# Attention scores: the low-key rotary product as two 64-row matmuls for two neighbouring score banks

## The reference, cut to what matters

```python
def mla_branch(cq, ckv, kr, z, g_q, w_uq, g_kv, w_ukv, cos, sin):
    ...
    def attend(blk):
        qn_i, qr_i = blk
        s = jnp.einsum('bqhd,bkhd->bhqk', qn_i, kn) + jnp.einsum('bqhr,bkr->bhqk', qr_i, kr)
        p = jax.nn.softmax(s.astype(jnp.float32), axis=-1).astype(v.dtype)
        return jnp.einsum('bhqk,bkhd->bqhd', p, v)
```

## Time and profile before

| | |
|---|---|
| median of 3 runs | 3331.22 us (3323.81, 3331.22, 3331.67) |
| the profiled execution, its time | 3325.03 us |
| its span in the profile | 3323.2 us |
| PE busy | 3091.8 us, 93% of the span |
| DVE, ACT, POOL busy | 41%, 35%, 20% |
| scores, first to last start of L1567 | 912.9 us to 1550.6 us |
| L1567 to L1571 | 256 matmuls each |

### The profile page before, as it was taken

One profiled execution on the slowest core, in us unless ns is written; L12 is line 12 of the kernel. 1 busy time (PEld: TensorE's weight loads), 2 busy tenths in 40 slices (PEclk: granted clock), 3 DMA queues, 4 the chain that ended last, 5 costly groups with the idle time before them and its releaser, 6 DMA issues.

```text
span 3323.2 us, 48512 instructions
## 1 busy us (share of the span) xinstructions
PE 3091.8 (93%) x17652; PEld 2611.1 (79%) x17652; DVE 1373.4 (41%) x2428; ACT 1158.3 (35%) x2089; POOL 655.4 (20%) x597
## 2 busy tenths in 40 slices
PE   4899999766899999999996999989999999999999
PEld 4668888656778888888786888868888888877887
DVE  5377777533567676775324111112222222222111
ACT  3552245433245555554225111123332333222110
POOL 2111211064212121221221000012121221112221
PEclk8999999887899999999998999999999999999999
DMA  6233354572411121211553111122121212135321
GB/s 216 77 118 99 111 165 157 202 232 63 116 36 57 45 60 42 63 51 59 170 165 127 70 73 73 47 79 76 57 76 57 76 57 76 57 109 170 101 89 62
DMA packets 261517, 318.50 MB, mean 96 GB/s; under 512 B 16851, under 2 KB 195283, under 8 KB 257908
## 3 DMA queue, kind: packets, MB, share of 16 engines
q1 hardware_dynamic: 261398, 316.89, 29.2%
HBM read 214.07 MB, written 102.76 MB: 95 GB/s over the span
## 4 chain that ended last, share of the span: by engine, by line
PE 83%; DVE 4%; POOL 3%; issue 3%; DMA 3%; ACT 3%; SPq 1%; POOLq 0%; DVEq 0%; ACTq 0%
PE PS L325 11%; PE PS L326 11%; PE PS L327 11%; PE PS L2117 4%; PE PS L2118 4%; PE PS L2119 4%; PE PS L2222 4%; PE PS L2224 3%; PE PS L2223 3%; PE PS L1578 3%; PE PS L1600 2%; PE PS L1601 2%; PE PS L1602 2%; PE PS L1567 2%; PE PS L2360 2%
## 5 line engine op out<-in xcount | busy, mean ns | idle before, releaser
L325 PE MATMUL PS<-hTh,whi 128*128 128x512 f32 x1664 | 660.9, 397 | 28.1 <-DVE hTl L281 14.5
L326 PE MATMUL PS<-hTl,whi 128*128 128x512 f32 x1664 | 652.0, 392 | 0.0
L327 PE MATMUL PS<-hTh,wlo 128*128 128x512 f32 x1664 | 651.9, 392 | 0.0
L325 PEld LDWEIGHTS PS<-hTh,whi 128*128 128x128 f32 x1664 | 315.2, 189 | 102.5 <-issue 18.1
L327 PEld LDWEIGHTS PS<-hTh,wlo 128*128 128x128 f32 x1664 | 315.1, 189 | 66.9
L326 PEld LDWEIGHTS PS<-hTl,whi 128*128 128x128 f32 x1664 | 315.5, 190 | 63.2
L317 POOL TENSOR_TENSOR whi<-wraw,zero 128x1024 fp32r<-128x1024 f32 x52 | 99.9, 1922 | 981.1 <-PE PS L327 953.0
L2117 PE MATMUL PS<-ow_h,of_h 128*128 128x512 f32 x576 | 225.0, 391 | 7.6 <-DVE oy L2074 7.6
L2118 PE MATMUL PS<-ow_l,of_h 128*128 128x512 f32 x576 | 224.8, 390 | 0.0
L2119 PE MATMUL PS<-ow_h,of_l 128*128 128x512 f32 x576 | 224.7, 390 | 0.0
L1676 ACT ACTIVATE pth<-PS 128x512 fp32r<-128x512 f32 x256 | 153.6, 600 | 187.5 <-PE PS L1578 187.5
(11 more groups left out here) (251 smaller groups left out, 6018.1 us busy)
## 6 DMA issues: line engine op xcount, KB each, us to landing
projT<-pev SPq DMA_DIRECT2D x80, 256.0 KB, 2.6
xt<-x SPq DMA_DIRECT2D x8, 2048.0 KB, 9.0
mw<-wmod SPq DMA_DIRECT2D x64, 256.0 KB, 2.8
oxt<-x SPq DMA_DIRECT2D x32, 512.0 KB, 4.8
sg_v<-vev SPq DMA_DIRECT2D x64, 256.0 KB, 2.3
wraw<-wuz SPq DMA_DIRECT2D x32, 512.0 KB, 5.9
vm<-sg_v SPq DMA_DIRECT2D x16, 1024.0 KB, 5.6
sgT<-mT SPq DMA_DIRECT2D x16, 1024.0 KB, 4.4
```

Source lines behind the costliest of these rows:

```text
L325: pe.matmul(PS[:, bank, :], w[1][:, s, k, :], hTh[:, k, b], start=(k == 0), stop=False)
L326: pe.matmul(PS[:, bank, :], w[1][:, s, k, :], hTl[:, k, b], start=False, stop=False)
L327: mm = pe.matmul(PS[:, bank, :], w[2][:, s, k, :], hTh[:, k, b], start=False, stop=(k == KD - 1))
```

## The change

`qsl` gets a fourth slice: the high part of the rotary query in both halves of the partitions. In the place of the fifth matmul of every bank stand, once for each pair of banks (0 and 1, 2 and 3), two matmuls of 64 rows: rows 0 to 63 into the even bank, rows 64 to 127 into the odd bank. They open the accumulation of both banks. So PE waits for the exponentials of both banks before the even one. The four other matmuls of a bank stay, and the fourth now releases `s_S`. The product low·low of the rotary parts is left out.

POOL gets a fourth instruction for each query block, and the counts of `s_q` go from 3 to 4. `qsl` grows by a third and moves to the place of `cql`, whose last reader comes before.

```diff
-        qsl = at("qsl", M0 + 165 * K, [P, 2, 3, P], F32R)
+        qsl = at("qsl", M0 + 64 * K, [P, 2, 4, P], F32R)
...
-                pe.wait_ge(s_q, N * 3 + 9)
+                pe.wait_ge(s_q, N * 4 + 12)
                 for b in banks:
-                    pe.wait_ge(s_exp, N * 4 + b + 1)
                     o, c = PS[:, b, :], blk(b)
-                    pe.matmul(o, qsl[:, u, 0, :], kh[:, c], start=True, stop=False)
+                    if b % 2 == 0:
+                        pe.wait_ge(s_exp, N * 4 + b + 2)
+                        for e in range(2):
+                            r = slice(ROPE * e, ROPE * e + ROPE)
+                            pe.matmul(PS[:, b + e, :], qsl[r, u, 3, :], krl[r, blk(b + e)], start=True, stop=False)
+                    pe.matmul(o, qsl[:, u, 0, :], kh[:, c], start=False, stop=False)
                     pe.matmul(o, qsl[:, u, 0, :], kl[:, c], start=False, stop=False)
                     pe.matmul(o, qsl[:, u, 1, :], kh[:, c], start=False, stop=False)
-                    pe.matmul(o, qsl[:, u, 2, :], krh[:, c], start=False, stop=False)
-                    pe.matmul(o, qsl[:, u, 2, :], krl[:, c], start=False, stop=True).then_inc(s_S, 1)
+                    pe.matmul(o, qsl[:, u, 2, :], krh[:, c], start=False, stop=True).then_inc(s_S, 1)
...
                 pool.wait_ge(s_S, N * 4 + 4)
-                pool.tensor_tensor(qsl[:, u, 0:3:2, :], qraw[:, u, :, :],
+                pool.tensor_tensor(qsl[:, u, 0:4:3, :], qraw[:, u, :, :],
                                    zero[:, 0:1].unsqueeze(1).broadcast_to([P, 2, P]), ALU.add).then_inc(s_q, 1)
-                pool.wait_ge(s_q, N * 3 + 7)
+                pool.wait_ge(s_q, N * 4 + 9)
+                pool.tensor_tensor(qsl[0:ROPE, u, 2, :], qraw[0:ROPE, u, 1, :],
+                                   zero[0:ROPE, 0:1].broadcast_to([ROPE, P]), ALU.add).then_inc(s_q, 1)
+                pool.wait_ge(s_q, N * 4 + 10)
                 pool.tensor_tensor(qsl[:, u, 1, :], qraw[:, u, 0, :], qsl[:, u, 0, :].bitcast(F32), ALU.subtract).then_inc(s_q, 1)
-                pool.wait_ge(s_q, N * 3 + 8)
-                pool.tensor_tensor(qsl[ROPE:P, u, 2, :], qraw[ROPE:P, u, 1, :], qsl[ROPE:P, u, 2, :].bitcast(F32), ALU.subtract
+                pool.wait_ge(s_q, N * 4 + 11)
+                pool.tensor_tensor(qsl[ROPE:P, u, 2, :], qraw[ROPE:P, u, 1, :], qsl[ROPE:P, u, 3, :].bitcast(F32), ALU.subtract
                                    ).then_inc(s_q, 1)
...
             def query(N, u):
-                sp.wait_ge(s_q, N * 3 + 3)
+                sp.wait_ge(s_q, N * 4 + 4)
```

More of the change, by code:

```diff
@@ L1810, in split @@
                 pool.wait_ge(s_S, N * 4 + 4)
-                pool.tensor_tensor(qsl[:, u, 0:3:2, :], qraw[:, u, :, :],
+                pool.tensor_tensor(qsl[:, u, 0:4:3, :], qraw[:, u, :, :],
                                    zero[:, 0:1].unsqueeze(1).broadcast_to([P, 2, P]), ALU.add).then_inc(s_q, 1)
-                pool.wait_ge(s_q, N * 3 + 7)
+                pool.wait_ge(s_q, N * 4 + 9)
+                pool.tensor_tensor(qsl[0:ROPE, u, 2, :], qraw[0:ROPE, u, 1, :],
+                                   zero[0:ROPE, 0:1].broadcast_to([ROPE, P]), ALU.add).then_inc(s_q, 1)
+                pool.wait_ge(s_q, N * 4 + 10)
                 pool.tensor_tensor(qsl[:, u, 1, :], qraw[:, u, 0, :], qsl[:, u, 0, :].bitcast(F32), ALU.subtract).then_inc(s_q, 1)
-                pool.wait_ge(s_q, N * 3 + 8)
-                pool.tensor_tensor(qsl[ROPE:P, u, 2, :], qraw[ROPE:P, u, 1, :], qsl[ROPE:P, u, 2, :].bitcast(F32), ALU.subtract
+                pool.wait_ge(s_q, N * 4 + 11)
+                pool.tensor_tensor(qsl[ROPE:P, u, 2, :], qraw[ROPE:P, u, 1, :], qsl[ROPE:P, u, 3, :].bitcast(F32), ALU.subtract
                                    ).then_inc(s_q, 1)
-                pool.wait_ge(s_q, N * 3 + 9)
+                pool.wait_ge(s_q, N * 4 + 12)
             def diagonal(N, I, u):
@@ L2251, in emit @@
         s_uu, E_uu = s_qi[1], 16 * NT * MH // 2
-        s_uz, E_uz = s_q, 6 + 3 * NT * MH
+        s_uz, E_uz = s_q, 8 + 4 * NT * MH
         s_um, E_um = s_S, 8 + 4 * NT * MH
@@ L2405, in _ @@
             latents_pool(pool)
-            pool.sem_inc(s_q, 6)
+            pool.sem_inc(s_q, 8)
             pool.sem_inc(s_dg, 2)
```

## The result

| | before | changed |
|---|---|---|
| median | 3329.12 us (4 runs) | 3348.56 us (4 runs, 3347.14 to 3350.34) |
| ratio | | 1.0062, 95% interval 1.0047 to 1.0077 |
| span of the profiled execution | 3323.2 us | 3347.3 us |

A forecast was written before the change was run, and what follows sets the result against it. The prediction took PE as the bound in the attention. Its terms, -29.7 + 0.9 + 49.9 + 1 = +22.1 us, on the median 3331.2 gave 3353 us, with an 8 in 10 range from 3337 to 3384 us.

The forecast's parts named there:

- The bound: In the attention, 912 to 1552 us, the time is the sum of PE's slots; PE is busy 630.0 of 640 us.
- One sign: PE's busy time was to fall or stay while its idle time before the pair and the next full matmul grows.
- The slot saved by the overlap: In the attention, each pair of 64-row matmuls takes one slot where two stood: 128 × 0.232 = 29.7 us less.
- the second half: The later start of a pair's second matmul, 7 ns for each of 128 pairs: 0.9 us more.
- The changes of shape: Between full matmuls and pairs, a late load 0.085 plus an open load 0.11, 0.195 us each, 256 times: 49.9 us more.
- One reading in support: Over all of L638, PE idles 8.6 us in 32 entries and exits, 0.27 each, of the same order as 0.195.
- The starting waits: At the start of the attention PE waits for second exponentials, 0.6 and 1.0 us later: 1 us more, between 0 and 1.6.
- The joint wait: In the loop, bank 0 waiting for two exponentials leaves 0.22 us after an odd block, and so costs nothing.
- rival 1: Changes of shape between 64 and 128 rows cost little, so the time is 3303 us; chance 0.09.
- POOL: One further 64x128 copy in each query block's split, 0.55 us, leaves 0.8 us to spare and costs nothing.
- The median: The sum is added to the runs' median 3331.2 us, 6.2 us above the profiled execution, giving 3353 us.

The follow-up runs named there:

- e9: Changed kernel with one full 128-row product in place of each pair (odd bank's left out) and each bank waiting for its own exponential: 3297.57 us, ratio 0.9915.
- e4: Changed kernel with each 64-row product alone, directly ahead of its own bank, so four changes of shape for two pairs' halves instead of two: 3426.98 us, ratio 1.0296.
- e3: Changed kernel with both products of a pair on rows 0 to 63: 3382.74 us, ratio 1.0157.
- e12: Changed kernel with the even bank's 64-row product alone, the odd bank's left out: 3349.68 us, ratio 1.0070.
- e5: Kernel before plus one tiny matmul ahead of each even bank, 64 rows, 128 columns of weights, 16 columns moving: 3376.55 us, ratio 1.0149.
- e6: Kernel before plus one tiny matmul ahead of each even bank, 128 rows, 128 columns of weights: 3341.55 us, ratio 1.0042.
- e8: Changed kernel with both pairs of a query block side by side ahead of bank 2, own waits for banks 0 and 1, DVE's low parts first: 3324.52 us, ratio 0.9987.
- e1: Changed kernel with the two 64-row products of a pair made full 128-row products in the same place, waits kept: 3324.66 us, ratio 0.9998.
- e2: Changed kernel with one full 128-row product into the even bank in place of each pair, odd bank's left out, joint wait kept: 3308.24 us, ratio 0.9943.
- e7: Kernel before plus one tiny matmul ahead of each even bank, 128 rows, 64 columns of weights, output partitions 0 to 63: 3338.43 us, ratio 1.0037.
- e10: Kernel before plus one tiny float32 matmul ahead of each even bank, 128 rows, 64 columns of weights, output partitions 64 to 127: 3374.45 us, ratio 1.0144.

## Why the prediction was right, point by point

**The bound.** PE is the bound in this stretch: e9 turns a saved slot into 0.22 us for each pair (28 us in all), e4 an added one with two changes into 0.61. One sign that the prediction gave was wrong: PE's busy time did not fall or stay, it rose from 3091.8 to 3118.2 us. A matmul with an open load is recorded from its load on (0.49 us in place of 0.39), so most of the loss counts as busy and only a part as idle.

**The slot saved by the overlap, 29.7 us.** Shown by e3 (a slot more on equal rows) and e12 (the second half all but free). For the second half I took 7 ns, from the quarter matmuls; the starts of the two lie 3 ns apart.

**The changes of shape, 49.9 us.** This is the term that decides, and it came from another stage of the same kernel, with other shapes. e5 and e6 confirm it alone, e4 and e8 by doubling and halving. In the changed kernel two blocks, with four pairs, last 19.63 us against 18.95: 0.171 for a pair, forecast 0.165. The price of the changes is right (two come to 0.39), and the rest is elsewhere: between 1200 and 1500 us the full score matmuls start 0.2328 apart on average where they started 0.2314 apart, 0.011 for the eight of a pair of banks. Why they do is not known. One reading in support was wrong: the 8.6 us in 32 times of the earlier trace rows are idle time of the weight load ahead of L638 alone, about half of them after full matmuls (0.35 each) and the others after L775 (0.17). They hold no way back to full matmuls, and so check one direction only.

**The Trainium skill**, page "TensorEngine Tiling (Array Packing)", section "Tiling Modes", Key Properties, has the drain on a change of the mode and not on a change of the tile alone. Runs here agree with both halves: 0.195 us for each change of rows (e5), and 0.003 between the starts of the two tiles of a pair in the changed kernel. The same page, section "Overview", has a speedup of up to 2x for 64 rows. That is there too, one slot for two (e12). For a lone pair the changes outweigh it: 0.39 against 0.225 us. Whether the late 0.09 is the drain itself, no run shows.

**The starting waits, 1 us.** e1 measures 0.9.

**The joint wait, nothing.** True for the changed kernel, but my step was wrong. I had looked at the start of the blocks that follow an odd one, found 0.22 us to spare and took it to stay, as nothing else changes. In the kernel before that was indeed the tighter case (0.29 after an even block). But the room depends on what PE does: with full products in the pair's place it falls to 0.05 after an even block (e1), and with one product less it is overdrawn there (e2). In the changed kernel, whose blocks are longer by the changes of shape, it is 0.27 after an even and 0.42 after an odd block. Had a change of shape been free, the gain would have been e2's 19 us and not the 28 of rival 1, which e9 reaches only with separate waits.

**POOL, nothing.** e1 confirms it; the new copy lasts 0.39 us, less than the 0.46 of the nearest row.

**The median.** I added the sum to 3331.2, the median of the three runs shown; the four runs now have 3329.1. 2 of the nearly 5 us between forecast and result are that.

**How much of the closeness is luck.** The mechanism is shown; the agreement to 0.1 us in the attention is not its merit. The slots that grew (1.4 us over 128 pairs) and the second half that cost less (0.5) work against each other, the first four blocks differ by microseconds without a known reason (50.3 us in the changed kernel, 53.0 in e12 with less work), and the medians differ by 19.4 us, not 22.

## What to carry to other kernels

A matmul of half the rows between full ones is dear twice: its weights were not loaded under the matmul before, nor were those of the one behind it, some 0.2 us each way here, almost a full slot of 512 columns. So count the changes of shape before the slots saved. With 512 columns, one pair between full matmuls saved 0.23 us and cost 0.39; two pairs side by side came out even (e8); three would gain some 0.3 us for a group (an estimate, 3 x 0.225 less 0.39; not run). And the price of a shape could be read here in another stage of the same kernel: look for the load that starts late after the last full matmul.

## What was not expected of the hardware

- Fewer columns of weights are not by themselves another shape. 64 columns with rounded operands to output partitions 0 to 63, between matmuls of 128 columns, kept the load at the start of the matmul before (e7, 11 us for 128 of them). As float32 the load was 0.09 us late, on partitions 64 to 127 (e10, 49 us) and also where the first product goes to 0 to 63 (L775 of the kernel before). Fewer rows cost also at row 0 (e5, and e12, whose only half is on rows 0 to 63).
- Two matmuls on the same 64 rows have their loads hidden as full ones have (e3), so the late load belongs to the change and not to the 64 rows.
- The open load of a 64-row matmul takes as long as that of 128 rows, 0.11 us for 128 columns. In e8 the second pair starts 0.34 after the recorded start of the first (0.73 less 0.39), 0.11 more than a slot.
